# An encoder layer with a mixture of experts on one core: slot tables and gathered rows in place of scattered rows and a combine

## The reference, cut to what matters

```
x = x + merged @ w_o
h = rmsnorm(x, norm_ffn)
group  = argmax(h @ w_router_group + b_router_group)               # 1 of 4
expert = top 2 of the 8 experts of that group, weights g_w * p / sum(p)
y[t]   = sum over its 2 experts: weight * ((silu(h[t] @ w_gate[e]) * (h[t] @ w_up[e])) @ w_down[e])
x = x + y
```

## Time and profile before

| | us |
|---|---|
| median of 3 runs (lowest, highest) | 2104.89 (2099.48, 2106.28) |
| the profiled execution, its own time | 2093.69 |
| its span | 2091.9 |

### The profile page before, as it was taken

One profiled execution on the slowest core, in us unless ns is written; L12 is line 12 of the kernel. 1 busy time (PEld: TensorE's weight loads), 2 busy tenths in 40 slices (PEclk: granted clock), 3 DMA queues, 4 the chain that ended last, 5 costly groups with the idle time before them and its releaser, 6 DMA issues. The chain is left out here.

```text
span 2091.9 us, 26160 instructions
## 1 busy us (share of the span) xinstructions
PE 1843.2 (88%) x9402; PEld 1412.4 (68%) x9402; DVE 1289.1 (62%) x1353; ACT 1019.4 (49%) x1579; POOL 597.4 (29%) x326
## 2 busy tenths in 40 slices
PE   4998999999999779999998997954999999999991
PEld 3777787787887654788787884432777666666660
DVE  2677866875885736333354361143888888888873
ACT  4234533643443430465674320113777777777761
POOL 5247646747655914010154320001000000000002
PEclk7999999999999888999999999976999999999995
DMA  3242342324434441554655343136999999999987
GB/s 107 65 126 89 116 139 87 117 91 121 123 101 136 139 153 48 157 178 150 190 189 168 126 136 133 61 150 239 376 379 387 375 369 370 375 371 364 363 337 259
DMA packets 248958, 416.40 MB, mean 199 GB/s; under 512 B 12128, under 2 KB 191840, under 8 KB 224160
## 3 DMA queue, kind: packets, MB, share of 16 engines
q1 hardware_dynamic: 244832, 400.41, 56.4%
q0 software_dynamic: 3456, 12.58, 1.6%
q10 hardware_dynamic: 576, 2.13, 0.3%
HBM read 337.03 MB, written 76.48 MB: 198 GB/s over the span
## 5 line engine op out<-in xcount | busy, mean ns | idle before, releaser
L2000 DVE TENSOR_TENSOR e_w_low<-e_raw,e_w_high 128x2048 fp32r<-128x2048 f32 x192 | 434.8, 2287 | 114.5 <-ACT e_w_high L1996 114.5
L1996 ACT ACTIVATE e_w_high<-e_raw 128x2048 fp32r<-128x2048 f32 x192 | 363.6, 1917 | 111.7 <-DMA e_raw<-in_w_up 35.8
L519 POOL TENSOR_TENSOR w_w_low<-w_raw,w_w_high 128x1024 fp32r<-128x1024 f32 x92 | 248.8, 2705 | 456.3 <-ACT w_w_high L514 456.3
L181 PE MATMUL bank<-h_high,w_w_high 128*128 128x512 f32 (+1 forms) x912 | 321.1, 352 | 31.8 <-ACT ssd_conv_in L798 16.7
L181 PE MATMUL bank<-h_low,w_w_high 128*128 128x512 f32 (+1 forms) x912 | 312.7, 343 | 0.0
L181 PE MATMUL bank<-h_high,w_w_low 128*128 128x512 f32 (+1 forms) x912 | 312.3, 342 | 0.0
L181 PEld LDWEIGHTS bank<-h_high,w_w_high 128*128 128x128 f32 x912 | 179.0, 196 | 64.5 <-issue 29.7
L2012 PE MATMUL bank<-e_w_high,e_xT_high 128*96 128x512 f32 x512 | 206.0, 402 | 8.4 <-DVE e_xT_low L2090 6.8
L2012 PE MATMUL bank<-e_w_high,e_xT_low 128*96 128x512 f32 x512 | 203.4, 397 | 0.0
L942 DVE SCALAR_TENSOR_TENSOR ssd_xc<-ssd_conv_in,ssd_conv_p,ssd_xc 128x774 f32<-128x774 f32 x144 | 196.5, 1364 | 10.8
L2012 PE MATMUL bank<-e_w_low,e_xT_high 128*96 128x512 f32 x512 | 202.1, 395 | 0.0
(11 more groups left out here) (277 smaller groups left out, 3536.3 us busy)
## 6 DMA issues: line engine op xcount, KB each, us to landing
e_raw<-in_w_gate SPq DMA_DIRECT2D x64, 1024.0 KB, 14.2
e_raw<-in_w_up SPq DMA_DIRECT2D x64, 1024.0 KB, 14.6
e_raw<-in_w_down SPq DMA_DIRECT2D x64, 1024.0 KB, 14.5
w_raw<-in_w_in SPq DMA_DIRECT2D x68, 512.0 KB, 3.9
ssd_decays<-decay_sums SPq DMA_DIRECT2D x48, 512.0 KB, 6.1
rows_in<-zeros SPq DMA_DIRECT2D x20, 768.0 KB, 9.0
projected<-ssd_side SPq DMA_DIRECT2D x33, 384.0 KB, 2.4
e_x<-rows_in SPq DMA_DIRECT2D x32, 384.0 KB, 15.4
```

The source lines that it names most:

```text
L181: last = pe.matmul(out, lhs[k][a], rhs[k][b], start=(k == 0 and m == 0), stop=(k == n - 1 and m == 2))
L519: pool.tensor_tensor(self.pair[u].low[:, :, :], self.raw[u][:, :, :], self.pair[u].high[:, :, :].bitcast(F32), ALU.subtract).then_inc(self ...
L1996: act.activation(pair[n].high[:, :], core.raw[c][:, :], ACT.Copy).then_inc(high_ok, 1)
L2000: dve.tensor_tensor(pair[n].low[:, :], core.raw[c][:, :], pair[n].high[:, :].bitcast(F32), ALU.subtract).then_inc(low_ok, 1)
```

## The change

**Slot tables.** For each assignment, DVE makes a one-hot row of its rank over the 96 slots (`at_slot`) and, for its expert, its token number and its weight (`of_expert`). PE multiplies the two (12 f32 matmuls of 96 x 64), which gives for each slot of each expert the token (`slot_row`) and the weight (`slot_weight`). From the token also come two tables of output rows, `slot_out`, one for each output tensor. An empty slot, and in `slot_out` a token of the other sequence, gets an index beyond the tensor; the transfers have a bound and leave such rows out.

**Rows.** h2 goes to DRAM tile by tile (SP). Each expert gathers its rows from there by an indirect transfer of POOL (`gather_rows`), in place of the 12 scatters and of SP's loads. `rows_in`, `rows_out`, the zero fills and the `combine` stage are gone.

**Outputs.** x1 is stored straight to the outputs in the mix. In `experts` POOL has a stream of its own (`pool_expert`): it gathers the output rows so far (two transfers, prompt and sample, the second behind the landing of the first), adds them to y, stores the sum back (two scatters), waits until they have landed, and gathers for the next expert. The weight is applied in `hidden` (a scalar per row). DVE makes the sum of the last expert.

**First chunks.** The order of SP's loads in the mix is new: w_o in four pieces of two k each, and the chunks of expert 0 ahead of the tiles' stores. Chunks 0 and 1 of expert 0 are split between the tiles (`round_early`, `lower_early`), and the same chunks of expert 1 are loaded behind tiles 4 and 5.

**Overflow.** The arithmetic that finds overflowing experts goes from the routing into DVE's stream behind expert 1 (`overflows`); its text is as before. `overflow_blocks` takes its rows by one-hot products; it is skipped as before.

The diff, cut to its core:

```diff
+                for j in range(4):
+                    ks = slice(2 * j, 2 * j + 2)
+                    sp.dma_start(wo[:, ks, :], w_view[:, ks, :]).then_inc(wo_in[j], 16)
+                for t in range(2):
+                    sp.dma_start(x[t][:, :], core.x_tile(t)).then_inc(x_in[t], 16)
+                sp.dma_start(gain_ffn[:, :], core.d["rows"][R_FFN:R_N].partition_broadcast(P)).then_inc(gain_in, 16)
+                sp.dma_start(wr[:, :, :], core.d["router"].rearrange("(k p) n -> p k n", p=P)).then_inc(wr_in, 16)
                 for c in range(CHUNKS):
                     load_chunk(sp, core, 0, c)
+                for t in range(NT):
+                    sp.wait_ge(x1_ok, t + 1)
+                    sp.dma_start(core.out_tile(t), x[t % 2][:, :]).then_inc(x1_out[t % 2], 16)
+                    sp.wait_ge(h2_ok, t + 1)
+                    sp.dma_start(core.h2_rows[t * P:(t + 1) * P, :], h2[t % 2][:, :]).then_inc(h2_out[t % 2], 16)
+                    if t + 2 < NT:
+                        sp.wait_ge(x1_out[t % 2], 16 * (t // 2) + 16)
+                        sp.dma_start(x[t % 2][:, :], core.x_tile(t + 2)).then_inc(x_in[t % 2], 16)
+                    if t >= NT - EARLY:
+                        c = t - NT + EARLY
+                        sp.wait_ge(core.e_low_ok, c + 1)
+                        load_chunk(sp, core, 1, c)
...
+                        round_early(act, core, t - NT + 1 + EARLY)
...
-                        pool.indirect_dma_start(
-                            out=core.rows_in[:, :],
-                            out_offset=bass.IndirectOffsetOnAxis(ap=core.place[:, n * NT + t:n * NT + t + 1], axis=0),
-                            in_=h2[:, t, :], in_offset=None).then_inc(scattered, 16)
-                pool.wait_ge(scattered, 2 * NT * 16)
+                for u in range(2):
+                    pool.wait_ge(h2_out[u], 16 * (NT // 2))
+                pool.wait_ge(slots_ok, 1)
+                for e in range(2):
+                    gather_rows(pool, core, e)
...
+                then(dve.tensor_tensor(of_expert[:, :, 0:NEXP], taken,
+                                       core.const[:, C_TOK:C_TOK + 2 * NT].unsqueeze(2).to_broadcast(pairs), ALU.mult))
...
+                then(dve.tensor_tensor(ranks[:, :, :], takes[:, :, :, :].rearrange("p n t e -> p n (t e)"),
+                                       core.bank[7][:, 0:NT * NEXP].unsqueeze(1).to_broadcast([P, 2, NT * NEXP]),
+                                       ALU.mult))
+                then(dve.tensor_reduce(core.rank[:, :], ranks[:, :, :].rearrange("p n (t e) -> p (n t) e", e=NEXP),
+                                       AX.X, ALU.add))
+                slots = [P, 2 * NT, CAP]
+                dve.tensor_tensor(at_slot[:, :, :], core.const[:, C_SLOT:C_SLOT + CAP].unsqueeze(1).to_broadcast(slots),
+                                  core.rank[:, :].unsqueeze(2).to_broadcast(slots), ALU.is_equal).then_inc(table_ok, 1)
...
+                then(dve.tensor_scalar(none[0][:, :], token, 0.0, NO_ROW, ALU.is_equal, ALU.mult))
+                dve.scalar_tensor_tensor(core.slot_row[:, :], token, -1.0, none[0][:, :],
+                                         ALU.add, ALU.add).then_inc(slots_ok, 1)
...
+                pe.wait_ge(table_ok, 1)
+                for j in range(2 * NT):
+                    last = pe.matmul(core.bank[5][0:CAP, 0:2 * NEXP], at_slot[:, j, :], of_expert[:, j, :],
+                                     start=(j == 0), stop=(j == 2 * NT - 1))
+                last.then_inc(table_mm, 1)
...
+def round_early(act, core, c):
+
+    act.wait_ge(core.raw_in[c], 16)
+    act.activation(core.pair[c].high[:, :], core.raw[c][:, :], ACT.Copy).then_inc(core.e_high_ok, 1)
+
+
+def lower_early(dve, core, c):
+
+    dve.wait_ge(core.e_high_ok, c + 1)
+    dve.tensor_tensor(core.pair[c].low[:, :], core.raw[c][:, :], core.pair[c].high[:, :].bitcast(F32),
+                      ALU.subtract).then_inc(core.e_low_ok, 1)
+
+
+def gather_rows(pool, core, e):
+
+    pool.indirect_dma_start(
+        out=core.e_x[e % 2][:, :], out_offset=None, in_=core.h2_rows[:, :],
+        in_offset=bass.IndirectOffsetOnAxis(ap=core.slot_row[:, e:e + 1], axis=0),
+        bounds_check=TOK - 1, oob_is_err=False).then_inc(core.e_x_in[e % 2], 16)
...
-            dve.tensor_tensor(hidden[u][:, :], silu[u][:, :], core.bank[UP][0:CAP, :], ALU.mult).then_inc(hidden_ok, 1)
+            dve.scalar_tensor_tensor(hidden[u][:, :], silu[u][:, :], core.slot_weight[:, bass.ds(e, 1)],
+                                     core.bank[UP][0:CAP, :], ALU.mult, ALU.mult).then_inc(hidden_ok, 1)
...
+        def pool_sofar(pool, e):
+            for n, (out, rows) in enumerate(zip(core.out, core.slot_out)):
+                if n:
+                    pool.wait_ge(sofar_in[e % 2], 32 * (e // 2) + 16)
+                pool.indirect_dma_start(
+                    out=sofar[e % 2][:, :], out_offset=None, in_=out[0, :, :],
+                    in_offset=bass.IndirectOffsetOnAxis(ap=rows[:, e:e + 1], axis=0),
+                    bounds_check=out.shape[1] - 1, oob_is_err=False).then_inc(sofar_in[e % 2], 16)
+
+        def pool_store(pool, e):
+            for out, rows in zip(core.out, core.slot_out):
+                pool.indirect_dma_start(
+                    out=out[0, :, :], out_offset=bass.IndirectOffsetOnAxis(ap=rows[:, e:e + 1], axis=0),
+                    in_=y[e % 2][:, :], in_offset=None,
+                    bounds_check=out.shape[1] - 1, oob_is_err=False).then_inc(y_out[e % 2], 16)
+
+        def pool_expert(pool, e, last=False):
+            u = e % 2
+            if e + 3 < NEXP:
+                pool.wait_ge(x_tr, e + 2)
+                gather_rows(pool, core, e + 3)
+            if not last:
+                pool.wait_ge(y_ok, e + 1)
+                pool.wait_ge(sofar_in[u], 32 * (e // 2) + 32)
+                pool.tensor_tensor(y[u][:, :], y[u][:, :], sofar[u][:, :], ALU.add).then_inc(sum_ok, 1)
+            pool.wait_ge(sum_ok, e + 1)
+            pool_store(pool, e)
+            pool.wait_ge(y_out[u], 32 * (e // 2) + 32)
+            if not last:
+                pool_sofar(pool, e + 1)
+
+        def overflows(dve):
...
+                dve_rows(dve, 0, 0)
...
+                overflows(dve)
...
+                dve.wait_ge(used, down(NEXP - 1, 1, True) + 1)
+                dve.wait_ge(y_out[1], 32 * LAST)
+                dve.wait_ge(sofar_in[1], 32 * LAST + 32)
+                for j in range(2):
+                    half = slice(j * 512, (j + 1) * 512)
+                    total = dve.tensor_tensor(y[1][:, half], core.bank[OUT + j][0:CAP, :], sofar[1][:, half], ALU.add)
+                total.then_inc(sum_ok, 1)
```

499 lines of the change are left out of this document (247 added, 252 removed).

## The result

| | before | after |
|---|---|---|
| time, median of 4 runs each | 2102.18 us | 2275.31 us |
| range | 2085.81 to 2106.28 | 2269.62 to 2291.1 |
| ratio of after to before, 95% interval | | 1.0851 [1.0771, 1.0931] |
| span of the profiled execution | 2091.9 us | 2267.8 us |

The change makes the kernel 8.5% slower. The forecast was 2058 us, 2% faster, with 2032 to 2108 as the range: the time lies far outside it.

The account below looks back on a forecast made before the run. Matmuls were taken to pace the expert stage early, the 16 DMA engines later. Terms -3 - 1 - 24 + 4 + 3 - 25 = -46 us gave 2047.7; for runs with a median 11.2 us higher, 2058 us, range 2032 to 2108.

Parts of the forecast that it names:

- POOL: one chain per expert: Expert stage: add, store and two so-far gathers in series, 4.85 + 3L, middle 19.0 us; 18.8 on average, +4 us.
- L: Issue-to-landing time of one indirect transfer in POOL's expert chain: 3.5 to 6.0 us, middle 4.7.
- The hops: Delays between the steps of POOL's chain per expert, 0.8 us in all.
- POOL's chain sets a clearly longer period: Rival, expert stage: indirect landings between weight packets; L of 5.5 gives period 21.35, 2137 us; chance 0.14 for slower.
- VectorE beside POOL: Expert stage: POOL's add slows DVE's work by 0 to 2.2 us per expert, up to 17.8 us.
- Mix, start: Start of the mix: w_o in four 1 MB loads lets PE start 3 us sooner, -3 us.
- Routing to the first expert: Between rank table and first expert matmul: two gathers replace twelve scatters, matmul at 1417.3 instead of 1441.64, -24 us.
- Overflow arithmetic: Moved from routing into DVE's stream behind expert 1: between 0 and 6.3 us, taken as +3.
- DMA per expert: Expert stage: 6.88 MB per expert at 367 GB/s, 18.75 us against 19.2 before.
- End: From y of expert 30 to the span's end: last chain, sum, store and overflow test replace the combine, -25 us.
- emptier L: End of the expert stage: landing of an indirect transfer taken as 4.2 us there.

Follow-up runs that it names:

- no_weights: Changed kernel with no weights loaded from expert 2 on (experts compute with those of expert 1); 2176.66 us, one run.
- no_low_no_weights: Changed kernel with no weights loaded after expert 1 and no lower parts of weights made by VectorE after the first four chunks; 2023.09 us, one run.
- no_low: Changed kernel with VectorE making no lower parts of the weights after the first four chunks, weight stream kept; 2226.98 us, one run.
- combine_kept: Changed kernel with y sent by SP to its own DRAM rows and gathers and sums at the end, as before the change; 2057.94 us, 0.9856 of before.
- packets_2k: Changed kernel with each 1 MB weight chunk as four loads with 2 KB packets in place of one with 8 KB; 2257.08 us, one run.

## Why the prediction was wrong

**The step that failed** is "POOL: one chain per expert". Its shape was right: an add, a store's issue and three landings in series, and once that is longer than the period it rules, with PE waiting at the turning of e_x. Two of its sizes were wrong, as the table of the chain shows.

- L, the landing. I took 4.7 us three times and gave 6.0 as the upper bound. The store had 4.7 in the mean, the two gathers 7.7 and 7.3; the mean of the three is 6.6. That is 5.6 us per expert. Both bounds came from the earlier trace rows, where the scatters and gathers run without the weight stream and without e_w_low. I wrote that no software-queue transfer runs beside the stream in this trace, and still took bounds from rows that could not contain the effect. A bound across such a gap would have been how other transfers fare in the stream: a weight load lands in 5.0 us at least and 14.4 in the median, 2.9 times as much. The same factor on the scatters' 4.6 gives 13 us, an estimate from above; the longest so-far gather took 11.9.
- The hops, which I had put at 0.8 us in all. An indirect issue of POOL starts 0.83 us behind the landing or the add that it waited for, three times per expert, and the add 0.15 us behind its landing: 2.6. The fixed part of the chain is 6.5 us where I had 4.85. Even with my L of 4.7 the period would have been 20.6 us and the time 31 x 1.94 = 60 us longer in place of 4: 2114 us, just outside the range.

With both, 6.5 + 3 x 6.6 = 26.2 us. The measured 25.5 is the mean over all experts, of which the first come faster.

**The range** failed with it. The rival "POOL's chain sets a clearly longer period" named the mechanism and the place, and the point from which it decides (L = 5.15; with the hops as measured it is 4.6), but had a chance of 0.14 and 2137 us for its price. The argument against it, that at a period of 20 us the DMA engines are at 94% and L sinks, is refuted: at 25.5 us, with the DMA share at 0.77 in 1600 to 1950 us, L was 6.6. A gather does not meet the mean load but a burst, since SP sends two chunks at a time: with no weights ahead the first packet came within 0.74 us, with 0.7 MB or more ahead in 3.1.

**VectorE beside POOL**: I costed what POOL does to VectorE (0 to 2.2 us per expert; measured 6 x 0.025 = 0.15). What VectorE does to POOL, the reverse, was left out, and it alone (no_weights) makes the spacing 22.6 us. The rule of the Trainium skill that I had weighed (GPSIMD Engine Reference, Specifications) names a contention of the two engines, and the runs agree that there is one; which of them pays it does not say, and here it is mostly GpSimd. The other rule of the Trainium skill, 2.0 us plus bytes over 436 GB/s (DMA: Bandwidth & Descriptors, Anatomy of one DMA), gave an estimate of 2.45 us for 48 rows. The x gather, which has 48 rows on average, lands in 4.4 us in the median without the stream (no_low_no_weights) and in 7.9 beside it (no_low); the so-far gathers, 24 rows each on average, in 3.7 and 7.5.

**The other terms**, at their places:

```profile
1266.77 2.18 SPq L1713 DMA_DIRECT2D mix_wo<-in_w_o  x4
1271.69 2.08 PE L1745 MATMUL bank<-mix_wo,mergedT 128*128 128x512 f32 x2 [8.07 <-DMA mix_wo<-in_w_o]
...
1400.49 0.56 DVE L1906 TENSOR_TENSOR r_ranks<-takes,bank 128x384 f32<-128x384 f32 x1
...
1407.56 0.19 DVE L1919 SCALAR_TENSOR_TENSOR slot_row<-bank,r_none 96x32 int32<-96x32 f32 x1
...
1408.78 1.22 POOL L1945 DMA_INDIRECT e_x<-h_rows,slot_row  x1 [27.55 <-issue]
...
1418.35 0.74 PE L2024 MATMUL bank<-e_w_high,e_xT_high 128*96 128x512 f32 x1 [1.64 <-DVE e_xT_low L2102]
```

- *Mix, start*: -3 us predicted. PE starts 4.92 us after the first load, before 7.97: -3.05.
- *Routing to the first expert*: the table steps took 2 us less than I had summed (ranks to slot table 7.1 for 9.0), the gather's landing and POOL's start more, and the first matmul comes 17.9 us behind the ranks where 17.5 was forecast. But the ranks themselves came 6 us later behind the mix, because of the early chunks that I had counted as reaching no one. From the first w_o load to the first expert matmul the gain is 172.8 - 151.6 = 21.2, for 27 in the two terms.
- *Overflow arithmetic*, +3, can't be told from POOL's chain in the changed kernel. In combine_kept, with the place arithmetic beside it, DVE is at it from 1459.31 to 1468.2 and PE then waits 7.6 us for e_w_low; the first five intervals are 20.1 us there for 17.9 later. Less the 2.3 us of the place arithmetic that is 5.3, nearer to the upper bound of 6.3 (whose own sum, 7.7 - 3.9 + 2.2, gives 6.0).
- *DMA per expert*, 18.75: the kernels that come near this limit have other values, at most 17.96 with one indirect transfer (383 GB/s) and 19.5 with three (352 GB/s); the 367 GB/s of the earlier trace rows belongs to before.
- *End*, -25 predicted. In the same terms, from y of expert 30 to the end of the span: 51.5 us before, 27 forecast, 39.3 measured (y at 2228.46), so -12. From the timeline of POOL after:

```profile
2234.47 2.93 POOL L2159 TENSOR_TENSOR e_y<-e_y,e_sofar 96x1024 f32<-96x1024 f32 x1 [2.99 <-DMA e_sofar<-out,slot_out]
2238.23 0.94 POOL L2146 DMA_INDIRECT out<-e_y,slot_out  x1 [0.84 <-POOL e_y L2159]
...
2243.52 0.98 POOL L2139 DMA_INDIRECT e_sofar<-out,slot_out  x1 [3.11 <-DMA out<-e_y,slot_out]
2247.84 0.97 POOL L2139 DMA_INDIRECT e_sofar<-out,slot_out  x1 [3.33 <-DMA e_sofar<-out,slot_out]
...
2255.39 0.94 POOL L2146 DMA_INDIRECT out<-e_y,slot_out  x1 [0.30 <-issue]
```

With the weights gone the landings are 3.2 to 4.1 us, and with the hops a step takes 4.0 to 4.3, near the emptier L of 4.2 that I had used without hops: two errors that cancel. From the add of expert 30 to the last store's issue 20.9 us pass, about as worked out (2.8 + 1.25 + 3 x 4.2 + 1.3 + 1.25 = 19.2). The miss has two main parts: the add of 30 starts 6.0 us behind its y, since the chain is behind, and from the last store's issue the span goes on for 12.4 us where I had counted 7.2. Of these 3.7 are the landing; the rest, 8.7 us, is the end of the stage and the overflow test, which I had put at 3.

## What to carry to other kernels

- A latency in a chain that closes on itself has to be bounded under the load that will run beside it. If the trace has no such transfer, the shortest and the median of quiet ones are both lower bounds, and the upper bound comes from whatever else lands in the busy stretch. Count the hop behind each wait as well: 0.83 us three times per expert would here have put the forecast out of its range alone.
- Where a read-modify-write runs from step to step, count the landings that stand in series and let the data dependence reach over two steps if it can: two sums instead of one, with three transfers instead of five, took 6.1 us off each period here. Better still, if the stage is also near the limit of its DMA engines, move the irregular transfers out of it, as the combine at the end does: 2058 us against 2092.
- An idle engine is not a free one. POOL was at zero in the stage before, but the issue of a so-far gather went from 0.96 to 2.9 us in the median and its add from 2.34 to 4.19 beside VectorE's two-input subtract (no_weights). A price has to be asked for in both directions.

## What the runs showed of the hardware

- A so-far gather (96 indices, of which 24 on average are rows of 4 KB in its output) lands in 3.7 us in the median with no weight stream (no_low_no_weights) and in 7.5 beside a stream of 1 MB loads (no_low), with the same issue of 0.98 us. The first packet of a so-far gather comes 0.57 us behind the issue in the one case and 2.8 in the other. 2 KB packets in place of 8 KB in the stream changed that wait by 0.3 to 0.4 us (packets_2k against after).
- The issue of an indirect transfer (0.94 to 0.98 us alone) takes up to 5.8 us beside VectorE's 128x2048 two-input subtract and the stream, up to 4.4 beside the subtract alone, and VectorE slows little in the mean (2.31 for 2.29 us in the changed kernel, 2.47 in no_weights); only where it meets POOL's add does it take up to 4.5.
- POOL starts an indirect issue 0.83 us behind the landing that it waited for (in after, no_low and no_weights alike), its add 0.15 us behind.
- Rows past the bound of an indirect transfer are not moved but leave a packet of 4 bytes of some 9 ns: 17920 packets on the software queue, of which 4608 have 4096 bytes (three for each of the 1536 rows) and 13312 have 4. By the count of slots 10752 of these are skipped rows, and 16 more come with each of the 160 transfers.
- With three indirect transfers per expert in place of one and a plain store, what all 16 DMA engines move goes from 383 to 352 GB/s at nearly the same busy share (0.98 and 1.00), and a weight packet takes 361 ns for 341.
